# Strassen-type block products in a decoder layer: activation sums made in place and earlier, weight sums made by adding DMA transfers

## The chip, the cores and the metric

The kernel runs on one core of one Trainium2 chip. The metric is the device time of one execution in microseconds (us).

## The reference

One layer with two token mixers, in float32, for 1024 tokens and a model width of 1024:

```python
h = rmsnorm(x, ln_pre)
(c_val, c_glu, c_gate, q, k, v, a_gate, g_conv, g_attn) = split_columns(h @ w_in)
u = c_val * sigmoid(c_glu)
c = silu(layernorm(depthwise_causal_conv31(u) + b_dw))
ya = (c @ w_pw * silu(c_gate)) @ w_br_conv
yb = (sliding_window_sink_attention(q, k, v) * silu(a_gate)) @ w_br_attn
m = sigmoid(g_conv) * ya + sigmoid(g_attn) * yb
x = x + rmsnorm(m @ w_out, ln_post)
x = x + sigmoid(x @ w_ple_gate) * (p @ w_ple_proj)
```

The change lies around one of these products, `c @ w_pw`.

## The kernel before

**Products.** Activations lie transposed, with features on the partitions (8 blocks of 128) and the 1024 tokens along the row. Every float32 operand is split into two parts, `hi` (ScalarE copies it to fp32r) and `lo` (VectorE subtracts `hi` from the original), and TensorE makes three passes, hi·hi, lo·hi and hi·lo. A tile is 128 output features by 1024 tokens: 8 blocks of K, 3 passes, 2 halves, 48 matmuls of 128x512. Its weights (512 KB) are loaded by SyncE into `w_raw` with two slots, split into `w_hi` and `w_lo`, and its result goes to one of two slots of the PSUM tensor `psg`. Tiles are numbered: E0 = 58 to 65 is the product with `w_br_attn` (operand `o_hi`, `o_lo`), G0 = 66 to 73 that with `w_br_conv` (operand `y_hi`, `y_lo`), then `w_out` and `w_ple_gate`.

**The seven products.** Between tile 65 and tile 66 stands `c @ w_pw`. It is done by Strassen's scheme in Winograd's form: for each of four pairs of output tiles (`i` = 0 to 3) seven half-size products instead of eight, in the order P1, P2, P6, Q5, P7, Q3, P4, which are numbered b = 7i + n with n = 0 to 6 (`seventh`, L901 to L923). Each has 12 matmuls. P1, P2 and P4 use quarters of the activations (`c_hi`, `c_lo`), the four others sums of quarters (`s_hi`, `s_lo`). P1, P2 and Q3 use a block of the weights as loaded (`pair_raw`, 1 MB for each pair, SyncE, L497), the others sums of two to four blocks.

**Who makes what in this stage.**
- `row_sum` (VectorE, L1869 to L1881): four sums of quarters, 128x2048 each, from `conv` into `s_raw`. `s_raw` and the parts made from it lie where `o_hi` and `o_lo` lie, the operands of tile 65, so the sums wait until that tile has used them (`o_used`, `tile_done`). `sum_high` (ScalarE, L1259) and `row_low` (VectorE, L1883) split them.
- `pair_sum` (VectorE, L1838): four sums of weight blocks for each pair, 128x512 each.
- `block_high` (ScalarE, L1247) and `block_low` (VectorE, L1856): the two parts of each of the 28 weight operands, into `pair_w` with six slots. A slot is free when the product six before (three before in the last pair) is done.
- `keep` (ScalarE, L1264): copies a product out of PSUM where the next product in its bank adds to a copy. P6 waits for keep(P1), P7 for keep(P6), Q3 for keep(Q5) and P4 for keep(P7) (`kept_ready`, L917).
- `take` (VectorE, L1888): combines products, multiplies by the gate and writes `y_raw`. `y_high` and `y_low` split `y_raw` for tile 66.
- `merge_row` (VectorE, L1829): takes the result of a tile of the stage before out of PSUM.

**What sets the order.** It is written out by hand: a list of calls for ScalarE (L1284 to L1330) and one for VectorE (L1908 to L1974), each executed strictly in order, each instruction with its semaphore waits. A call that waits holds back all calls behind it on its engine. In the loop over b from 7 to 27, the `keep` calls of finished products (`made_since`) stand between the `block_high` calls. GpSimd has no work between 723 and 990 us of the span.

## Time and profile before

| | us |
|---|---|
| median of 3 runs | 1168.77 (1167.45 to 1169.88) |
| the profiled execution | 1169.1 |
| its span, first to last instruction | 1167.3 |
| TensorE busy in the span | 1152.7 (99%) |
| mean granted clock of TensorE | 0.995 of full speed |

The span stands for one execution; 1.8 us of that execution's time lie around it. Engines are PE (TensorE), PEld (its weight loads), DVE (VectorE), ACT (ScalarE), POOL (GpSimd) and SP (SyncE). "L919" is line 919 of the kernel. The number in brackets behind an instruction is the time its engine was idle before it, with what released it. "x2" means two instructions merged into one row, with the time from the start of the first to the end of the second.

### The profile page before, as it was taken

The page shows a single profiled execution, that of the slowest core. Times are in us where ns is not written, and L with a number is a line of the kernel's source. Part 1 is how long each engine was busy: PE and PEld are TensorE (multiplying, and loading weights), DVE is VectorE, ACT ScalarE, POOL GpSimd, SP SyncE. Part 2 cuts the span into 40 slices and gives each one's busy share as a digit, 9 for nine tenths or more (in the row PEclk, how much of TensorE's full clock was granted, in tenths as well). Part 3 has the DMA queues.
Part 4 walks back from the last instruction along what each step waited for, and adds up shares of the span by engine and source line. Part 5 has one row for each costly group of instructions (what it writes and reads, how often), then busy time and mean ns, then how long its engine had stood idle before and what let it go on. Part 6 is the DMA issues. An engine that isn't in the chain of part 4 may idle for free.

```text
span 1167.3 us, 16052 instructions
## 1 busy us (share of the span) xinstructions
PE 1152.7 (99%) x6256; PEld 938.7 (80%) x6256; DVE 900.1 (77%) x1025; ACT 398.8 (34%) x711; POOL 18.0 (2%) x16
## 2 busy tenths in 40 slices
PE   9999999999999999999999999999799999999998
PEld 7888888888888888877777888888687888888887
DVE  6999999999999984699886787867856444357776
ACT  6431221221221121366665433433334212344342
POOL 2020000000000000000000000000000000000000
PEclk9999999999999999999999999999899999999999
DMA  9622222222222323211212111453315432434565
GB/s 350 274 90 72 62 82 72 68 76 72 72 72 72 99 54 86 54 56 56 74 55 75 36 54 50 119 209 109 118 63 171 171 108 75 141 109 144 174 204 180
DMA packets 37408, 124.87 MB, mean 107 GB/s; under 512 B 4688, under 2 KB 5456, under 8 KB 36848
## 3 DMA queue, kind: packets, MB, share of 16 engines
q1 hardware_dynamic: 25840, 86.48, 23.0%
q10 hardware_dynamic: 11520, 37.75, 9.4%
q8 instruction: 30, 0.49, 0.2%
q14 instruction: 18, 0.15, 0.0%
HBM read 96.30 MB, written 25.17 MB: 104 GB/s over the span
## 4 chain that ended last, share of the span: by engine, by line
PE 93%; DVE 4%; ACT 2%; issue 1%; DMA 1%; ACTq 0%; SPq 0%; DVEq 0%
PE psg L555 72%; PE psg L847 6%; PE psb L919 5%; PE psg L579 2%; PE psb L761 1%; PE psg L818 1%; PE psg L662 1%; PE psg L608 1%; DVE s_raw L1881 1%; PE psg L779 1%; ACT probs L1134 1%; PE psg L813 1%; PE psb L662 1%; DMA p_raw<-pT 1%; PE psg L944 0%
## 5 line engine op out<-in xcount | busy, mean ns | idle before, releaser
L555 PE MATMUL psg<-h_hi,w_hi 128*128 128x512 f32 x768 | 236.9, 390 | 0.0
L555 PE MATMUL psg<-h_lo,w_hi 128*128 128x512 f32 x768 | 236.5, 389 | 0.0
L555 PE MATMUL psg<-h_hi,w_lo 128*128 128x512 f32 x768 | 236.4, 389 | 0.0
L1409 DVE TENSOR_TENSOR w_lo<-w_raw,w_hi 128x1024 fp32r<-128x1024 f32 x105 | 128.4, 1223 | 89.7 <-ACT w_hi L990 84.9
L555 PEld LDWEIGHTS psg<-h_hi,w_hi 128*128 128x128 f32 x768 | 143.9, 188 | 30.5 <-issue 0.8
L555 PEld LDWEIGHTS psg<-h_lo,w_hi 128*128 128x128 f32 x768 | 144.2, 188 | 29.9
L555 PEld LDWEIGHTS psg<-h_hi,w_lo 128*128 128x128 f32 x768 | 144.2, 188 | 29.9
L990 ACT ACTIVATE w_hi<-w_raw 128x1024 fp32r<-128x1024 f32 x104 | 110.0, 1058 | 165.0 <-PE psg L555 138.2
L1586 DVE SCALAR_TENSOR_TENSOR conv<-u,cols,conv 128x1024 f32<-128x1024 f32 x120 | 154.3, 1286 | 0.0
L1586 DVE SCALAR_TENSOR_TENSOR work<-u,cols,work 128x1024 f32<-128x1024 f32 x112 | 145.8, 1301 | 0.0
L847 PE MATMUL psg<-h_hi,w_hi 128*128 128x512 f32 x128 | 51.8, 405 | 0.0
L847 PE MATMUL psg<-h_hi,w_lo 128*128 128x512 f32 x128 | 49.9, 390 | 0.0
L847 PE MATMUL psg<-h_lo,w_hi 128*128 128x512 f32 x128 | 49.9, 390 | 0.0
L555 PE MATMUL psg<-x_hi,w_hi 128*128 128x512 f32 x120 | 46.7, 389 | 0.0
L555 PE MATMUL psg<-x_hi,w_lo 128*128 128x512 f32 x120 | 46.7, 389 | 0.0
L555 PE MATMUL psg<-x_lo,w_hi 128*128 128x512 f32 x120 | 46.7, 389 | 0.0
L555 PE MATMUL psg<-m_hi,w_hi 128*128 128x512 f32 x112 | 43.7, 390 | 0.0
L555 PE MATMUL psg<-m_lo,w_hi 128*128 128x512 f32 x112 | 43.6, 389 | 0.0
L555 PE MATMUL psg<-m_hi,w_lo 128*128 128x512 f32 x112 | 43.6, 389 | 0.0
L1980 DVE SCALAR_TENSOR_TENSOR work<-ring,psg 128x1024 f32<-128x1024 f32 x8 | 9.8, 1221 | 43.5 <-PE psg L555 38.8
L555 PE MATMUL psg<-y_hi,w_hi 128*128 128x512 f32 x128 | 40.0, 394 | 2.7 <-DVE w_lo L1409 2.7
L919 PE MATMUL psb<-s_hi,pair_w 128*128 128x512 f32 x128 | 39.7, 391 | 1.1 <-DVE pair_w L1864 1.1
(285 smaller groups left out, 1812.9 us busy)
## 6 DMA issues: line engine op xcount, KB each, us to landing
w_raw<-weights SPq DMA_DIRECT2D x106, 512.0 KB, 3.5
gates<-ring ACTq DMA_DIRECT2D x24, 512.0 KB, 2.7
ring<-gates ACTq DMA_DIRECT2D x24, 512.0 KB, 4.0
x_rows<-x_rows SPq DMA_DIRECT2D x8, 512.0 KB, 9.9
conv<-xT SPq DMA_DIRECT2D x8, 512.0 KB, 14.1
ple<-ple_out SPq DMA_DIRECT2D x8, 512.0 KB, 13.2
merged<-merged_out ACTq DMA_DIRECT2D x8, 512.0 KB, 5.3
pair_raw<-w_pairs SPq DMA_DIRECT2D x4, 1024.0 KB, 6.1
```

The lines of the kernel that those rows point to most:

```text
L555: mm = nc.tensor.matmul(psg[:, slot, h * HALF:(h + 1) * HALF], w[:, wslot, (wk + k) * P:(wk + k + 1) * P], r[:, k, h * HALF:(h + 1) * HALF ...
L579: mm = nc.tensor.matmul(psg[:, slot, h * HALF:(h + 1) * HALF], w[:, slot, k * P:(k + 1) * P], r[:, k, h * HALF:(h + 1) * HALF], start=(k = ...
L608: mm = nc.tensor.matmul(psg[:, slot, cols_h], w[:, slot, k * P:(k + 1) * P], r[:, k, cols_h], start=(k == 0 and n == 0), stop=(k == KT - 1 ...
L662: mm = nc.tensor.matmul(out, w[:, t // 4, cols_k], r[:, k, h * HALF:(h + 1) * HALF], start=(k == 0 and n == 0), stop=(k == PLE_KT - 1 and ...
L761: mm = nc.tensor.matmul(psb[out_rows, 2 * jp + par, j2 * 2 * P + first:j2 * 2 * P + first + width], qo[rows, 4 * g + 2 * jp + j2, queries] ...
L779: mm = nc.tensor.transpose(psg_banks[:, bank, first + h * HD:first + h * HD + HD], probs[g][queries, 4 * jp + h, :], ident[queries, queries])
L813: nc.tensor.matmul(out_of(p, side, par), vstep[rows, n - 1, gs], heads_of(pt_prev[rows], par), start=True, stop=False)
L847: mm = nc.tensor.matmul(gate_bank(p), w[:, t % 2, k * P:(k + 1) * P], r[:, k, half], start=(k == 0 and m == 0), stop=(k == KT - 1 and m == 2))
L919: mm = nc.tensor.matmul(psb[:, pair_bank(i, n), :], pair_w[:, at_w, w, k * P:(k + 1) * P], r[:, block_of, k, :], start=(not onto and k == ...
L990: nc.scalar.activation(w_hi[:, j % 2, :], w_raw[:, j % 2, :], ACT.Copy).then_inc(w_hi_ready, 1)
L1409: nc.vector.tensor_tensor(w_lo[:, slot, :], w_raw[:, slot, :], w_hi[:, slot, :].bitcast(F32), ALU.subtract).then_inc(w_lo_ready, 1)
L1586: own.step(stt(dst, src[:, j:j + S], tap(j), dst, ALU.mult, ALU.add))
```

## The change

1. **Activation sums in place.** `s_raw` is gone. The four `row_sum` calls write over the quarters of `conv` themselves, after the parts of `conv` have been made (`lo_ready` 3·KT), and so no longer wait for tile 65. They move ahead of tile 65, two before the `merge_row` of tile 63 and two before that of tile 64. Only the splits (`sum_high`) wait for tile 65's operands. The sums are used in the order P6, Q5, P7, Q3 as they are split. `c_high(7)` and `c_low(7)` move forward by one tile.
2. **Boundary steps reordered.** The lists of ScalarE and VectorE between tile 65 and b = 7 are written anew. The merge of tile 65 and the load of the second gate row now come before the splits of weights 4 to 6. At the end of the stage the split of tile 66's weights moves forward, to behind b = 24 (ScalarE) and b = 25 (VectorE), and the waits of `y_high` on products are one lower for two of four pairs.
3. **Weight sums by adding transfers.** `pair_sum` and its 16 instructions on VectorE are gone. GpSimd issues DMA transfers from the memory to four buffers of 128x512 (256 KB each): the first of a sum copies a block, each later one adds a block to what is there (`accum_op`). A pair needs 11 of them, 4 copies and 7 additions: P6 one copy and two additions, Q5 and P7 one and one, P4 one and three. Each addition waits for the transfer before it into the same buffer, each copy for the `block_low` that read the buffer for the pair before. All 44 transfers stand in one list on GpSimd's queue, the first behind `ln_scaled`.

```diff
-        s_raw = at("s_raw", [4, KP, HALF], F32, RD)
...
+        SUM_OF = {Q5: 0, P6: 1, P7: 2, P4: 3}
+        ADDENDS = ((0, 1), (0, 1, 3), (1, 3), (0, 1, 3, 2))
...
+        upper, lower = slice(0, HALF), slice(HALF, S)
+        def sum_of(n):
+            return conv[:, slice(KP, KT) if n in (1, 3) else slice(0, KP), upper if n in (0, 3) else lower]
...
+            def sum_step(i, n, step):
+                t = SUM_OF[n]
+                if step == 0 and i > 0:
+                    pool.wait_ge(pair_lo, 7 * (i - 1) + n + 1)
+                if step > 0:
+                    pool.wait_ge(sum_loaded[t], 16 * (len(ADDENDS[t]) * i + step))
+                op = ALU.bypass if step == 0 else ALU.add
+                pool.dma_start(pair_sums[t][:], WPW[:, i, ADDENDS[t][step], :], accum_op=op).then_inc(sum_loaded[t], 16)
+            pool.wait_ge(ln_scaled, KT)
+            for i in range(PAIRS):
+                sum_step(i, P6, 0)
+                sum_step(i, Q5, 0)
+                sum_step(i, P6, 1)
+                sum_step(i, Q5, 1)
+                sum_step(i, P6, 2)
+                sum_step(i, P7, 0)
+                sum_step(i, P4, 0)
+                sum_step(i, P7, 1)
+                sum_step(i, P4, 1)
+                sum_step(i, P4, 2)
+                sum_step(i, P4, 3)
             rsqrt(3, slice(0, NB // 2))
...
-                    act.wait_ge(pair_summed, 4 * i + {Q5: 1, P6: 2, P7: 3, P4: 4}[n])
-                    src = pair_sums[:, {Q5: 0, P6: 1}[n], :] if n in (Q5, P6) else pair_t[:, pair_slot(b), 1, :]
+                    t = SUM_OF[n]
+                    act.wait_ge(sum_loaded[t], 16 * len(ADDENDS[t]) * (i + 1))
+                    src = pair_sums[t][:]
...
-                act.wait_ge(s_made, n + 1)
-                nc.scalar.activation(s_hi[:, n], s_raw[:, n], ACT.Copy, scale=0.5).then_inc(s_hi_ready, 1)
+                act.wait_ge(s_made, 4)
+                if n < 3:
+                    act.wait_ge(o_used, n + 1)
+                else:
+                    act.wait_ge(tile_done, G0 + KT)
+                nc.scalar.activation(s_hi[:, n], sum_of(n), ACT.Copy, scale=0.5).then_inc(s_hi_ready, 1)
...
-                act.wait_ge(product_made, LAST_PAIR + (4, 4, 6, 6)[k // 2])
+                act.wait_ge(product_made, LAST_PAIR + (3, 4, 5, 6)[k // 2])
...
                 block_high(b)
+                if b == LAST_PAIR + Q5:
+                    high(G0 // 2 - 1, 2)
...
+                s2, s1, s3, s4 = (sum_of(j) for j in range(4))
+                a, b, op = {1: (s3, s1, ALU.subtract), 2: (s2, s3, ALU.subtract),
+                            0: (s1, s2, ALU.subtract), 3: (s4, s2, ALU.add)}[n]
+                dve.wait_ge(lo_ready, 3 * KT)
...
                 block_low(b)
+                if b == LAST_PAIR + P7:
+                    tile_low(G0)
             y_low(0)
             y_low(1)
+            take(PAIRS - 1, 1)
             y_low(2)
+            take(PAIRS - 1, 2)
             y_low(3)
-            take(PAIRS - 1, 1)
-            tile_low(G0)
-            take(PAIRS - 1, 2)
-            y_low(4)
-            y_low(5)
             take(PAIRS - 1, 3)
-            y_low(6)
-            y_low(7)
+            for k in range(KP, KT):
+                y_low(k)
...
-    nc = bacc.Bacc("TRN2", target_bir_lowering=False, num_devices=1, dynamic_dma_scratch_size=1024)
+    nc = bacc.Bacc("TRN2", target_bir_lowering=False, num_devices=1, dynamic_dma_scratch_size=2048)
```

VectorE from the merge of tile 63 on, before (`merged_out` is the merge of a tile, `s_raw` a row sum, `s_lo` its split, `pair_w` a block_low):

```order
L1836 SCALAR_TENSOR_TENSOR merged_out<-ring,psg 128x1024 [waits merged_spilled1,gate_loaded1,tile_done]
L1409 TENSOR_TENSOR w_lo<-w_raw,w_hi 128x1024 [waits w_hi_ready]
L1823 SCALAR_TENSOR_TENSOR c_lo<-conv,c_hi 128x2x512 [waits hi_ready]
L1853 TENSOR_TENSOR pair_sums<-pair_raw_83 128x512 [waits pair_loaded0]
L1853 TENSOR_TENSOR pair_sums<-pair_sums,pair_raw_83 128x512 [waits pair_summed,pair_loaded0]
L1836 SCALAR_TENSOR_TENSOR merged_out<-ring,psg 128x1024 [waits merged_spilled0,gate_loaded0,tile_done]
L1864 TENSOR_TENSOR pair_w<-pair_raw_83,pair_w 128x512 [waits pair_hi] x2
L1881 TENSOR_TENSOR s_raw<-conv 128x2048 [waits o_used]
L1881 TENSOR_TENSOR s_raw<-s_raw,conv 128x2048 [waits s_made,o_used]
L1886 SCALAR_TENSOR_TENSOR s_lo<-s_raw,s_hi 128x2048 [waits s_hi_ready]
L1881 TENSOR_TENSOR s_raw<-conv,s_raw 128x2048 [waits s_made,o_used]
L1886 SCALAR_TENSOR_TENSOR s_lo<-s_raw,s_hi 128x2048 [waits s_hi_ready]
```

The same place in the changed kernel (the in-place sums read `conv<-conv`, 128x4x512):

```order
L1860 SCALAR_TENSOR_TENSOR c_lo<-conv,c_hi 128x2x512 [waits hi_ready] x2
L1895 TENSOR_TENSOR conv<-conv 128x4x512 [waits lo_ready]
L1895 TENSOR_TENSOR conv<-conv 128x4x512 [waits s_made,lo_ready]
L1873 SCALAR_TENSOR_TENSOR merged_out<-ring,psg 128x1024 [waits merged_spilled1,gate_loaded1,tile_done]
L1446 TENSOR_TENSOR w_lo<-w_raw,w_hi 128x1024 [waits w_hi_ready]
L1895 TENSOR_TENSOR conv<-conv 128x4x512 [waits s_made,lo_ready] x2
L1873 SCALAR_TENSOR_TENSOR merged_out<-ring,psg 128x1024 [waits merged_spilled0,gate_loaded0,tile_done]
L1884 TENSOR_TENSOR pair_w<-pair_raw_83,pair_w 128x512 [waits pair_hi] x2
L1900 SCALAR_TENSOR_TENSOR s_lo<-conv,s_hi 128x2048 [waits s_hi_ready]
L1884 TENSOR_TENSOR pair_w<-pair_sums_115,pair_w 128x512 [waits pair_hi]
L1900 SCALAR_TENSOR_TENSOR s_lo<-conv,s_hi 128x2048 [waits s_hi_ready] x2
L1873 SCALAR_TENSOR_TENSOR merged_out<-ring,psg 128x1024 [waits merged_spilled1,gate_loaded1,tile_done]
```

All four row sums now stand ahead of the merge of tile 64, and no addition of weight blocks is left on VectorE.

ScalarE of the changed kernel from the split of weight 7 on (`pair_w` is a block_high, of b = 7 and 8, 9, 10, 11, 12, 13; `kept` are keep(P7 of pair 0) and keep(P1 of pair 1); `pair_sums_115` is the buffer of P6, 114 that of Q5, 116 that of P7, 117 that of P4):

```order
L1289 ACTIVATE pair_w<-pair_raw_84 128x512 [waits pair_loaded1,product_made] x2
L1289 ACTIVATE pair_w<-pair_sums_115 128x512 [waits sum_loaded1,product_made]
L1308 ACTIVATE kept<-psb 128x512 [waits quarter_read,product_made]
L1289 ACTIVATE pair_w<-pair_sums_114 128x512 [waits sum_loaded0,product_made]
L1289 ACTIVATE pair_w<-pair_sums_116 128x512 [waits sum_loaded2,product_made]
L1289 ACTIVATE pair_w<-pair_raw_84 128x512 [waits pair_loaded1,product_made]
L1308 ACTIVATE kept<-psb 128x512 [waits quarter_read,product_made]
L1358 DMA ring<-gates 128x1024 [waits y_made]
L1358 DMA ring<-gates 128x1024
L1289 ACTIVATE pair_w<-pair_sums_117 128x512 [waits sum_loaded3,product_made]
```

The sequence of calls is that of before, but four of them for each pair now wait for a DMA transfer (`sum_loaded`) where they waited for VectorE (`pair_summed`), and `kept` stands behind the one for P6.

GpSimd of the changed kernel, the 11 transfers of pair 1 (before, its queue is empty here):

```order
L993 DMA pair_sums_115<-w_pairs 128x512 [waits pair_lo]
L993 DMA pair_sums_114<-w_pairs 128x512 [waits pair_lo]
L993 DMA pair_sums_115<-w_pairs 128x512 [waits sum_loaded1]
L993 DMA pair_sums_114<-w_pairs 128x512 [waits sum_loaded0]
L993 DMA pair_sums_115<-w_pairs 128x512 [waits sum_loaded1]
L993 DMA pair_sums_116<-w_pairs 128x512 [waits pair_lo]
L993 DMA pair_sums_117<-w_pairs 128x512 [waits pair_lo]
L993 DMA pair_sums_116<-w_pairs 128x512 [waits sum_loaded2]
L993 DMA pair_sums_117<-w_pairs 128x512 [waits sum_loaded3] x3
```

The queue is served in this order, so an addition that waits for its forerunner holds back all the others.

## Rows read from the trace of the kernel before

**Rows 1.** The page: busy time by engine over the span.

```profile
PE 1152.7 (99%) x6256; PEld 938.7 (80%) x6256; DVE 900.1 (77%) x1025; ACT 398.8 (34%) x711; POOL 18.0 (2%) x16
```

**Rows 2.** Busy time by stretch: engines in order, granted clock, DMA share, GB/s.

```profile
core 0: us, PE busy (x) PEld busy (x) DVE busy (x) ACT busy (x) POOL busy (x), PEclk, DMA share, GB/s
...
810.30:829.50 19.20, 17.12 (x73) 13.09 (x71) 17.63 (x16) 8.15 (x11) 0.00 (x0) 1.00 0.05 12
829.50:838.70 9.20, 4.99 (x13) 3.97 (x14) 7.56 (x12) 2.84 (x6) 0.00 (x0) 0.63 0.59 204
838.70:893.00 54.30, 54.30 (x241) 44.95 (x240) 31.10 (x45) 20.07 (x33) 0.00 (x0) 1.00 0.26 89
...
895.80:904.50 8.70, 5.96 (x20) 4.69 (x20) 7.46 (x10) 2.40 (x3) 0.00 (x0) 0.80 0.86 275
```

**Rows 3.** TensorE in order of time: start, duration, instruction, idle before it.

```profile
810.33 0.62 PE L919 MATMUL psb<-c_hi,pair_w 128*128 128x512 f32 x2
...
822.72 0.73 PE L919 MATMUL psb<-s_hi,pair_w 128*128 128x512 f32 x2 [1.12 <-DVE pair_w L1864]
...
833.71 1.19 PE L919 MATMUL psb<-c_hi,pair_w 128*128 128x512 f32 x2 [5.18 <-ACT kept L1272]
...
838.61 0.63 PE L919 MATMUL psb<-c_hi,pair_w 128*128 128x512 f32 x2
...
893.04 0.62 PE L919 MATMUL psb<-c_hi,pair_w 128*128 128x512 f32 x2
...
898.67 0.70 PE L555 MATMUL psg<-y_hi,w_hi 128*128 128x512 f32 x2 [2.74 <-DVE w_lo L1409]
...
904.46 0.62 PE L555 MATMUL psg<-y_hi,w_hi 128*128 128x512 f32 x2
```

**Rows 4.** VectorE in order of time, 773 to 825 us.

```profile
773.56 1.22 DVE L1809 TENSOR_TENSOR conv<-conv,sums 128x1024 f32<-128x1024 f32 x1
...
788.77 1.22 DVE L1836 SCALAR_TENSOR_TENSOR merged_out<-ring,psg 128x1024 f32<-128x1024 f32 x1 [5.38 <-PE psg L555]
...
799.65 1.22 DVE L1836 SCALAR_TENSOR_TENSOR merged_out<-ring,psg 128x1024 f32<-128x1024 f32 x1 [5.97 <-PE psg L555]
...
803.70 2.28 DVE L1881 TENSOR_TENSOR s_raw<-conv 128x2048 f32<-128x2048 f32 x1
...
822.59 2.28 DVE L1886 SCALAR_TENSOR_TENSOR s_lo<-s_raw,s_hi 128x2048 fp32r<-128x2048 f32 x1
824.79 0.68 DVE L1864 TENSOR_TENSOR pair_w<-pair_raw,pair_w 128x512 fp32r<-128x512 f32 x1
```

**Rows 5.** ScalarE in order of time, 800 to 834 us.

```profile
806.02 1.92 ACT L1262 ACTIVATE s_hi<-s_raw 128x2048 fp32r<-128x2048 f32 x1 [3.04 <-DVE s_raw L1881]
...
829.61 1.15 ACT L1257 ACTIVATE pair_w<-pair_raw 128x512 fp32r<-128x512 f32 x2 [2.81 <-DVE merged_out L1836]
...
832.99 0.58 ACT L1272 ACTIVATE kept<-psb 128x512 f32<-128x512 f32 x1
```

**Rows 6.** VectorE in order of time, 890 to 900 us.

```profile
893.60 2.36 DVE L1418 SCALAR_TENSOR_TENSOR y_lo<-y_raw,y_hi 128x1024 fp32r<-128x1024 f32 x2 [0.97 <-ACT y_hi L1279]
...
897.20 1.22 DVE L1409 TENSOR_TENSOR w_lo<-w_raw,w_hi 128x1024 fp32r<-128x1024 f32 x1
```

**Rows 7.** DMA issues of the whole run: size, median us from issue to landing.

```profile
w_raw<-weights SPq DMA_DIRECT2D x106, 512.0 KB, 3.5
...
x_ring<-xT ACTq DMA_DIRECT2D x16, 256.0 KB, 3.4
...
pack<-qo SPq DMA_DIRECT2D x12, 64.0 KB, 2.3
```

**Rows 8.** DMA issues between 803 and 832 us, same columns.

```profile
merged<-merged_out ACTq DMA_DIRECT2D x1, 512.0 KB, 7.4
```

**Rows 9.** The DMA queue of SyncE, 803 to 832 us.

```profile
827.56 0.33 SPq L497 DMA_DIRECT2D pair_raw<-w_pairs  x1
```

**Rows 10.** GpSimd, groups by line: busy us, mean ns of one.

```profile
L962 POOL TENSOR_TENSOR rstd<-mean_sq,expo 128x4 f32<-128x4 f32 x3 | 3.1, 1020 | 405.7 <-DVE mean_sq L1423 387.5 <-DVE mean_sq L1453 18.2
```

More of the change, by code:

```diff
@@ L158, in build @@
         quarter = at("quarter", [HALF], F32, G + 14 * KB)
-        pair_sums = at("pair_sums", [2, HALF], F32, G + 16 * KB)
+        pair_sums = [at(f"pair_sums{t}", [HALF], F32, G + (16, 18, 32, 34)[t] * KB) for t in range(4)]
         sums = at("sums", [S], F32, G + 16 * KB)
@@ L180, in build @@
         v_last = cols[:, COL_TAPS:COL_TAPS + P]
-        assert small <= G + 24 * KB and G + 32 * KB <= nc.sbuf_usable_end
+        assert small <= G + 24 * KB and G + 36 * KB <= nc.sbuf_usable_end
         psg = ctx.enter_context(nc.psum_tensor("psg", [P, 2, S], F32))
@@ L269, in build @@
         pair_loaded = [sem("pair_loaded0"), sem("pair_loaded1")]
-        pair_summed = sem("pair_summed")
+        sum_loaded = [sem(f"sum_loaded{t}") for t in range(4)]
         pair_hi = sem("pair_hi")
@@ L907, in seventh @@
                     pe.wait_ge(lo_ready, 3 * KT)
[L908 to L909 removed]
+                if i == 0 and n in (P6, Q5, P7, Q3):
+                    pe.wait_ge(s_ready, {P6: 1, Q5: 2, P7: 3, Q3: 4}[n])
                 if i > 1 and n == P1:
@@ L1836, in merge_row @@
                 stt(merged_out[:, j, :], ring[:, j, :], 1.0, psg[:, j, :], ALU.add, ALU.mult).then_inc(ps_free[j], 1)
-            def pair_sum(i, n):
-                blocks = pair_raw[i % 2]
-                dve.wait_ge(pair_loaded[i % 2], 16 * (i // 2 + 1))
-                if n == Q5:
-                    out, a, b = pair_sums[:, 0, :], blocks[:, 0, :], blocks[:, 1, :]
-                elif n == P6:
-                    dve.wait_ge(pair_summed, 4 * i + 1)
-                    out, a, b = pair_sums[:, 1, :], pair_sums[:, 0, :], blocks[:, 3, :]
-                elif n == P4:
-                    from_slot(dve, 7 * i + n)
-                    out, a, b = pair_t[:, pair_slot(7 * i + n), 1, :], pair_sums[:, 1, :], blocks[:, 2, :]
-                else:
-                    from_slot(dve, 7 * i + n)
-                    out, a, b = pair_t[:, pair_slot(7 * i + n), 1, :], blocks[:, 1, :], blocks[:, 3, :]
-                nc.vector.tensor_tensor(out, a, b, ALU.add).then_inc(pair_summed, 1)
             def block_low(b):
@@ L1926, in _ @@
             block_low(1)
-            row_sum(0)
-            row_sum(1)
             row_low(0)
-            row_sum(2)
+            block_low(2)
             row_low(1)
-            block_low(2)
-            row_sum(3)
+            row_low(2)
+            merge_row(KT - 1)
             block_low(3)
-            pair_sum(0, P7)
             row_low(3)
+            take(0, 0)
             block_low(4)
-            row_low(2)
             block_low(5)
-            pair_sum(0, P4)
             block_low(6)
-            merge_row(KT - 1)
-            take(0, 0)
             for b in range(7, 7 * PAIRS):
```

55 lines of the change are left out of this document (19 added, 36 removed).

## The prediction

> **What bounds the kernel.** I read the busy shares first: TensorE is busy 99% of the span, 1152.7 of 1167.3 us [rows 1]. An edit off TensorE can therefore win only what TensorE loses in idle time, or at a lowered clock, and 14.6 us of idle time are all there is. The busy time by stretch shows where that lies near the change: TensorE idles 2.1 us between 810.3 and 829.5, 4.2 us up to 838.7 and 2.7 us between 895.8 and 904.5, while the 54.3 us between are full [rows 2]. The granted clock is 1.00 (the 2.4 GHz level) in the first and third stretch, and 0.63 and 0.80 in the other two, so part of the time there was at 1.2 GHz.
>
> TensorE's own rows give the sizes [rows 3]. In the full stretch 20 products take 893.04 − 838.61 = 54.43 us, 2.72 each. The first pair of tiles runs from 810.33 to 838.61, 28.28 us for seven products that need 7 × 2.72 = 19.04: 9.24 us lost. Of these, 1.12 are a wait for a weight split on VectorE and 5.18 a wait for `kept`; behind the latter the product at 833.71 takes 4.90 us instead of 2.72, because the clock had fallen after the idle time. The last product ends at 893.04 + 2.72 = 895.76, tile 66 starts at 898.67 after a wait for `w_lo`, and its fourth block of K, due 3 × 1.36 = 4.08 us after 895.76, comes at 904.46: 4.62 us lost. Together **13.9 us**.
>
> The causes are on the two engines with lists. VectorE does four row sums of 2.28 us after 803.7, and is still at the splits at 822.59 [rows 4]; it merges tile 65 only then, ScalarE waits for that merge until 829.61 with the later splits and the `kept` copy at 832.99 queued behind [rows 5], and that copy releases the product at 833.71. At the end `w_lo` stands behind four `y_lo` splits and ends at 898.4 [rows 6].
>
> **Part 1, sums in place and sooner.** Two row sums and one `c_lo` (2 × 2.28 by the row of a sum, 1.22 for the split, together 5.8 us) go ahead of the merge at 788.77, which had 5.38 us of idle time before it; two sums (4.5) go ahead of the merge at 799.65, which had 5.97 and loses two weight sums besides [rows 4]. The first merge may come 0.3 us late; TensorE needs its slot only one tile later, so I charge nothing. If that cover were gone, the price would be what exceeds the 10.9 us of a tile (4 × 2.72).
>
> After tile 65 I walk through the new lists. Behind the merge that starts at 799.65 and two DMA issues, ScalarE splits three weight blocks in some 0.55 each (two took 1.15) from 801.8, and row sums in 1.92 each from 803.4 [rows 5]. VectorE splits of 2.2 (822.59 to 824.79) then end at 807.5, 810.3, 812.5 and, behind the merge of tile 65 and block_low(3) (done at 814.3), at 816.5 [rows 4]. The products that use them are due at 815.8, 818.5, 821.2 and 823.9. block_low(4) ends at 818.4 against 821.2. The tightest spare is 2.8 us. So all 9.24 us go, if the weight sums arrive.
>
> **Part 2, the end of the stage.** `w_hi` and `w_lo` of tile 66 are now made behind splits 24 and 25, several microseconds ahead of 895.76, and `y_lo` of block k is needed only at 895.76 + 1.36 k, where VectorE needs 1.2 us each. All 4.62 us go.
>
> **Part 3, adding transfers.** VectorE loses 16 sums of 0.69 us; it has idle time there, so nothing on the path. What is added is a chain on GpSimd's queue, and no row shows one: GpSimd issued no transfer before, and no transfer added.
>
> Prices. *Issue*: SyncE's takes 0.33 us [rows 9], GpSimd's smallest two-operand instruction 1.02 [rows 10]; I take 1.0, since the same engine has to prepare 128 rows. *Copy* of 256 KB, issue to landing: 2.3 us for 64 KB and 7.4 for a transfer in a crowded stretch are the ends [rows 7, 8]; I take 3.4, the row of the same size. *Addition*: the same ends; I take the copy plus the time for reading a second 256 KB, by (3.5 − 2.3) / 448 KB × 256 KB = 0.7, so 4.1 us.
>
> The Trainium skill (Collectives: The Full Stack, the section on the bandwidth ceiling) says that a reducing transfer is slowed by reading two sources and not by the addition. No run here shows it yet; a doubling of the data part alone is what my 0.7 supposes.
>
> The queue is served in order, so one pair takes: P6 copy 3.4, first P6 addition 4.1, issue 1.0, P7 copy 3.4, issue 1.0, P4 additions 4.1 and 4.1, issue 1.0. That is **22.1 us for each pair, against 19.04 that TensorE takes**. The chain thus falls behind by 3.1 us a pair, from a lead it has at the start.
> - Pair 0: issued from the last `ln_scaled` at 774.8 [rows 4] on, landed by some 801, needed from 802 on, the last after 819. No wait.
> - Pair 1: the second transfer, a copy for Q5, waits for block_low(3) at 814.3 and holds back the rest. P6 is summed at 814.4 + 1.0 + 4.1 + 4.1 = 823.6. ScalarE then splits it (0.5) and copies P7 (0.5): `kept` stands ready at 824.7, P4 is due at 810.33 + 6 × 2.72 = 826.65. No wait. The turn ends at 834.1.
> - Pair 2: P6 summed at 834.1 + 3.4 + 8.2 = 845.7, `kept` at 846.8, P4 of pair 1 due at 845.7: **1.1 us**. P4's sum lands at 859.3, and keep(P6) behind it at 860.9 against 860.4: **0.5 us**.
> - Pair 3: turn from 856.2, P6 summed at 867.8, `kept` at 868.9, P4 of pair 2 due at 866.3: **2.5 us**, and behind a wait of that size the clock falls: 4.90 − 2.72 = 2.2 and 4.62 − 2.91 = 1.7 were lost at the lower level [rows 3], so **2.0**. P4's sum lands at 881.4, due at about 892.
>
> **The sum**: 1169.1 (the profiled execution: span 1167.3 and 1.8 around it; 0.3 above the median of 1168.77) − 13.9 + 1.1 + 0.5 + 2.5 + 2.0 = 1161.3. Against the median 1161.0.
>
> **Rivals.**
> - *The chain keeps up.* With a turn under 20 us no product waits. A copy of 2.8 (between the rows of 64 and 512 KB) and an addition of 3.5 give 5.6 + 10.5 + 3.0 = 19.1. Then 1169.1 − 13.9 = 1155.2. For it: the DMA engines are busy only 26% between 838.7 and 893 [rows 2]. Against it: 33 transfers of 262 kB add 8.7 MB to the 4.8 MB of these 54 us, and the additions read their target too. The Trainium skill (DMA: Bandwidth & Descriptors, the section on the anatomy of one DMA from gpsimd) gives 2.0 us plus bytes over 436 GB/s, an estimate of 2.6 us for a copy here; by that the sum would be this rival's. No run here shows it yet.
> - *Slower: keep(P7) behind the weight split.* ScalarE cannot copy P7 out of its bank before it has split the next pair's P6 sum, and TensorE's P4 waits for that copy. With additions of 6.1 us (a little above half way from 4.1 to the crowded 7.4) P6 of pair 1 is summed at 827.6, P4 of pair 0 waits 2.0 us, and a turn takes 28.1: by the same walk four more waits of 2.5 us follow, each behind the same kind of wait, and all five drop the clock. 12 + 5 × 2.0 = 22 us, against 13.9 saved: 1177.2. It decides from additions of about 5.3 us on (turn 25.7). For it: transfers compete with 1 MB of `pair_raw` and 1 MB of gates in each pair, and a transfer in such company took 7.4 [rows 8]. Against it: that one wrote to memory, and twice the data. With 7.4 for an addition the same walk gives 1189.
> - *The change doesn't do all it says.* If sums in place held a merge up by a tile or the boundary kept a wait, some microseconds of 9.24 would stay. The walk shows 2.8 us spare; small.
>
> **Chances.** The chain a little late, as in my sum: 0.35. It keeps up: 0.27. Additions near 5.3 us, both effects cancelling: 0.11. Slower through late sums: 0.24. A boundary wait that stays: 0.03. A change of 0.2%, 2.3 us, is about what a measurement can tell from none. Faster 0.64, same 0.12, slower 0.24. The likeliest case alone spans 1156 to 1166. The range goes from 1154.5, the rival without any wait less a little, to 1178, the slower rival; additions beyond some 6.1 us are left out, with a chance of about 0.13.
>
> **What would show it.** In the changed kernel's profile the waits at P7 of pair 0 (1.12), P4 of pair 0 (5.18) and tile 66 (2.74) should be gone, and four row sums should stand before 800 us. GpSimd's transfers of `pair_sums` should land 3.4 to 4.1 us after issue and repeat every 22 us; waits on `kept` should be seen at P4 of pairs 1 and 2, with ScalarE's `pair_w` of P6 released by a DMA. No such waits at all would mean the first rival, a wait already at P4 of pair 0 the second. I would be wrong altogether if TensorE waited for `s_lo` or if the merge of tile 63 moved by more than a microsecond.

## The result and the profile after

The changed kernel takes **1184.47 us** (median of 4 executions, 1183.57 to 1186.32) against 1169.09 for the kernel before in the same series: a ratio of 1.0135, 95% interval 1.0118 to 1.0153. It is slower by 15.4 us, and 1161.0 with a range up to 1178 had been forecast. The profiled execution took 1186.32 us with a span of 1184.5, 17.2 above the span of before.

The page of the changed kernel, the lines that answer to [rows 1] and [rows 7], and TensorE's waits in the stage:

```profile
PE 1159.9 (98%) x6256; PEld 942.9 (80%) x6256; DVE 889.6 (75%) x1009; ACT 398.4 (34%) x711; POOL 52.3 (4%) x60
...
L926 PE MATMUL psb<-s_hi,pair_w 128*128 128x512 f32 x128 | 42.5, 415 | 6.5 <-ACT kept L1308 6.5
L926 PE MATMUL psb<-c_hi,pair_w 128*128 128x512 f32 x96 | 34.6, 446 | 13.0 <-ACT kept L1308 13.0
...
pair_sums<-w_pairs POOLq DMA_DIRECT2D x44, 256.0 KB, 5.3
```

The same matrix work is now busy for 7.2 us longer (1159.9 against 1152.7), which is lowered clock, and 19.5 us of idle time stand before the products, all of it behind `kept`. The 44 transfers land a median 5.3 us after issue.

The stage by stretch, with the columns of [rows 2], two of six stretches and the sum of all:

```profile
810.30:829.40 19.10, 16.58 (x74) 13.39 (x72) 10.82 (x12) 7.35 (x11) 4.37 (x6) 1.00 0.81 215
...
860.00:880.00 20.00, 16.74 (x60) 13.30 (x60) 5.77 (x9) 3.92 (x7) 4.68 (x6) 0.83 0.65 163
...
sum 107.20, PE 87.70 PEld 69.88 DVE 43.70 ACT 31.65 POOL 25.00; mean PE 14.62 PEld 11.65 DVE 7.28 ACT 5.28 POOL 4.17
```

TensorE in order of time, answering to [rows 3]: the first product, the fifth and the seventh (P7 and P4 of pair 0), P4 of pair 3, and tile 66.

```profile
810.40 0.62 PE L926 MATMUL psb<-c_hi,pair_w 128*128 128x512 f32 x2
...
821.28 0.62 PE L926 MATMUL psb<-s_hi,pair_w 128*128 128x512 f32 x2
...
830.25 0.70 PE L926 MATMUL psb<-c_hi,pair_w 128*128 128x512 f32 x2 [3.37 <-ACT kept L1308]
...
913.18 1.17 PE L926 MATMUL psb<-c_hi,pair_w 128*128 128x512 f32 x2 [3.17 <-ACT kept L1308]
...
917.59 0.62 PE L562 MATMUL psg<-y_hi,w_hi 128*128 128x512 f32 x2
```

From 810.40 to 917.59 the 28 products take 107.2 us where 28 × 2.72 = 76.2 are needed: **31.0 us are lost**, against 13.9 before. The difference of 17.1 is the whole difference of the spans (17.2), so nothing of the loss lies elsewhere. TensorE is busy 87.7 of the 107.2 us: 19.5 us are idle (six waits, of 3.37, 4.62, 4.46, 1.87, 2.02 and 3.17 us) and 11.5 are work at a lowered clock (0.83 to 0.91 in the mean of each stretch from 829.4 us on, where the steady part of before has 1.00).

Parts 1 and 2 did what they should. The fifth product comes in step (810.40 + 4 × 2.72 = 821.28), where the first pair of before had its first wait; tile 66 starts without one. What is left is part 3. ScalarE in order of time shows the wait that releases P4 of pair 0:

```profile
829.00 0.63 ACT L1289 ACTIVATE pair_w<-pair_sums 128x512 fp32r<-128x512 f32 x1 [5.88 <-DMA pair_sums<-w_pairs]
829.53 0.58 ACT L1308 ACTIVATE kept<-psb 128x512 f32<-128x512 f32 x1
...
837.62 0.82 ACTq L1358 DMA_DIRECT2D ring<-gates  x2
```

The split of pair 1's P6 sum waits 5.88 us for its DMA, and the copy of P7, done by TensorE at 824.0, stands behind it until 829.53. The other waits are of two kinds. Those at P4 of pairs 1 and 2 are like this one. Those at P7 of pairs 1 and 2 and at P4 of pair 3 stand behind the split of a P4 sum: in pair 1 it waits 10.37 us for its DMA (848.57), with keep(P6) behind it at 849.63. And GpSimd's queue in order of time shows why the sums are late (each row is one to three issues; in brackets the landing that let them go):

```profile
808.09 1.45 POOL L993 DMA_DIRECT2D pair_sums<-w_pairs  x2 [4.62 <-DMA pair_sums<-w_pairs]
814.74 1.50 POOL L993 DMA_DIRECT2D pair_sums<-w_pairs  x2 [5.21 <-DVE pair_w L1884]
...
837.96 0.86 POOL L993 DMA_DIRECT2D pair_sums<-w_pairs  x1 [6.22 <-DMA pair_sums<-w_pairs]
844.32 2.00 POOL L993 DMA_DIRECT2D pair_sums<-w_pairs  x3 [5.50 <-DMA pair_sums<-w_pairs]
850.23 1.81 POOL L993 DMA_DIRECT2D pair_sums<-w_pairs  x2 [3.90 <-DMA pair_sums<-w_pairs]
857.14 2.00 POOL L993 DMA_DIRECT2D pair_sums<-w_pairs  x3 [5.11 <-DMA pair_sums<-w_pairs]
863.46 1.82 POOL L993 DMA_DIRECT2D pair_sums<-w_pairs  x2 [4.31 <-DMA pair_sums<-w_pairs]
870.35 0.86 POOL L993 DMA_DIRECT2D pair_sums<-w_pairs  x1 [5.06 <-DMA pair_sums<-w_pairs]
874.92 1.99 POOL L993 DMA_DIRECT2D pair_sums<-w_pairs  x3 [3.71 <-DMA pair_sums<-w_pairs]
880.52 1.85 POOL L993 DMA_DIRECT2D pair_sums<-w_pairs  x2 [3.62 <-DMA pair_sums<-w_pairs]
885.01 2.00 POOL L993 DMA_DIRECT2D pair_sums<-w_pairs  x3 [2.63 <-DMA pair_sums<-w_pairs]
891.74 1.82 POOL L993 DMA_DIRECT2D pair_sums<-w_pairs  x2 [4.73 <-DMA pair_sums<-w_pairs]
900.19 0.86 POOL L993 DMA_DIRECT2D pair_sums<-w_pairs  x1 [6.63 <-DMA pair_sums<-w_pairs]
904.65 0.88 POOL L993 DMA_DIRECT2D pair_sums<-w_pairs  x1 [3.60 <-DMA pair_sums<-w_pairs]
```

A turn of the chain, from the last addition of one pair's P4 to that of the next, takes 36.2 us at first (with 5.21 of waiting for the `block_low` that frees Q5's buffer), then **30.6** (844.32 to 874.92) and 29.7 (874.92 to 904.65), against 19.04 for TensorE's seven products. It consists of five hops, each from one release to the next. Beside the prediction's terms for the same hops, the differences of neighbouring rows are:

| hop | of the same list in flight beside it | forecast | second turn | third turn |
|---|---|---|---|---|
| copy for P6 | P4's last addition, the copy for Q5 | 4.4 | 5.91 | 5.60 |
| first addition for P6 | the addition for Q5 | 4.1 | 6.91 | 4.49 |
| copy for P7 | P6's second addition, the copy for P4 | 4.4 | 6.32 | 6.73 |
| first addition for P4 | the addition for P7 | 5.1 | 6.89 | 8.45 |
| second addition for P4 | none | 4.1 | 4.57 | 4.46 |
| turn | | 22.1 | 30.6 | 29.7 |

In these two turns every row is let go by a landing, none by a `block_low`, so the buffers hold nothing up. The one addition with nothing of the list beside it is 0.4 us dearer than forecast; of the eight hops in company, seven are 1.2 to 3.4 us dearer. Other loads may weigh on it too: in the first turn the last hop took 844.32 − 837.96 = 6.36 us, where ScalarE had just issued 1 MB of gates (837.62); no run changes these loads alone.

Set against the chain, the loss reads as follows. P4 of pair 0 was due at 810.40 + 6 × 2.72 = 826.72, 18.6 us behind the issue of its last addition (808.09); P4 of pair 3 starts 8.5 us behind its own (913.18, 904.65). So 10.1 us of lead are used up. The three turns take 96.6 us where TensorE needs 57.1, 39.4 more. 39.4 − 10.1 = 29.3, and the last product takes 4.41 us instead of 2.72 at the lowered clock: 31.0. This balance must close whatever the cause, since it only splits the time between two products.

So it is a reading, not yet a proof: an addition may be dear for itself, and the order of the lists or the buffers may hold the chain. The experiments take it apart.

### The profile page after: what moved, and what is told of

Read it like the earlier page. It is cut to its first block, busy times and chain, and to the rows that moved or that the text cites. A ratio compares the mean times of both kernels' runs of the same rounds, so it can differ in the third digit from the quotient of the medians.

```text
span 1184.5 us, 16074 instructions
## 1 busy us (share of the span) xinstructions
PE 1159.9 (98%) x6256; PEld 942.9 (80%) x6256; DVE 889.6 (75%) x1009; ACT 398.4 (34%) x711; POOL 52.3 (4%) x60
## 4 chain that ended last, share of the span: by engine, by line
PE 88%; DMA 7%; DVE 2%; ACT 1%; issue 1%; POOL 0%; ACTq 0%; SPq 0%; DVEq 0%; POOLq 0%
PE psg L562 71%; PE psg L854 6%; DMA pair_sums<-w_pairs 6%; PE psb L926 2%; PE psg L586 2%; PE psb L768 1%; PE psg L825 1%; DMA conv<-xT 1%; PE psg L615 1%; PE psg L786 1%; ACT probs L1165 1%; PE psg L820 1%; DVE s_lo L1900 1%; PE psg L951 0%; PE psg L669 0%
## 5 line engine op out<-in xcount | busy, mean ns | idle before, releaser
L1884 DVE TENSOR_TENSOR pair_w<-pair_sums,pair_w 128x512 fp32r<-128x512 f32 x16 | 11.0, 689 | 58.4 <-ACT pair_w L1289 58.4
L926 PE MATMUL psb<-s_hi,pair_w 128*128 128x512 f32 x128 | 42.5, 415 | 6.5 <-ACT kept L1308 6.5
L926 PE MATMUL psb<-c_hi,pair_w 128*128 128x512 f32 x96 | 34.6, 446 | 13.0 <-ACT kept L1308 13.0
L993 POOL DMA_DIRECT2D pair_sums<-w_pairs x44 | 34.3, 923 | 222.4 <-DVE conv L1846 126.3
```

Source lines behind the costliest of these rows:

```text
L926: mm = nc.tensor.matmul(psb[:, pair_bank(i, n), :], pair_w[:, at_w, w, k * P:(k + 1) * P], r[:, block_of, k, :], start=(not onto and k == ...
L993: pool.dma_start(pair_sums[t][:], WPW[:, i, ADDENDS[t][step], :], accum_op=op).then_inc(sum_loaded[t], 16)
```

## The experiments

All were run beside the kernel before. Theory A: parts 1 and 2 give back the 13.9 us, and the chain of transfers is the bound and costs 31. The rivals: the moved steps cost something that the chain hides; adding transfers disturb other engines or loads by themselves; the chain is late through its order, through buffers, or through the order on ScalarE.

### Weight sums on VectorE again, parts 1 and 2 kept

The 44 transfers are gone; VectorE forms the four sums of a pair in one go, those of pair 0 ahead of the merge of tile 64, the later ones behind the last `block_low` of the pair before.

```diff
...
+            def pair_sums_of(i):
+                blocks = pair_raw[i % 2]
+                dve.wait_ge(pair_loaded[i % 2], 16 * (i // 2 + 1))
+                if i > 0:
+                    dve.wait_ge(pair_lo, 7 * i)
+                for n, a, b in ((Q5, blocks[:, 0, :], blocks[:, 1, :]), (P6, pair_sums[0][:], blocks[:, 3, :]),
+                                (P7, blocks[:, 1, :], blocks[:, 3, :]), (P4, pair_sums[1][:], blocks[:, 2, :])):
...
                 block_low(b)
+                if b % 7 == P4 and b < LAST_PAIR:
+                    pair_sums_of(b // 7 + 1)
```

> The changed kernel with part 3 undone: the weight sums are made by VectorE again, the four of a pair together behind the split of P4 of the pair before, into the changed kernel's four buffers. Parts 1 and 2 stay. Theory A (the chain of landings on GpSimd's queue is the whole loss): all waits of the stage go, 13.9 us less than before, about 1155 us, ratio 0.988. Rival B (parts 1 and 2 do not save what the walk says, for instance because VectorE is late again with four more sums before tile 64's merge): a wait of some microseconds stays at P7 or P4 of the first pair, 1158 to 1164.

Measured: 1155.42 us (1154.78 to 1155.75), ratio 0.9885 (0.9868 to 0.9901), span 1153.0. The first stretch of its stage:

```profile
810.30:829.40 19.10, 19.10 (x86) 15.81 (x85) 17.48 (x23) 9.28 (x15) 0.00 (x0) 1.00 0.35 111
```

TensorE is busy every microsecond, at a clock of 1.00. The span is 14.3 us under that of before, and the median 13.4 us under that of its own series (1168.81), around the 13.9 that parts 1 and 2 were to win. Part 3, put on top of them, costs 1184.47 − 1155.42 = 29 us by the medians, 31.5 between the two profiled spans. This version beats both kernels.

### The old boundary lists, and the old end of the stage

Two kernels made from the one above, each with one piece of the reordering undone. In the first, the lists of ScalarE and VectorE between tile 65 and b = 7 stand in the order of before the change, without the row sums and weight sums that stood there (the cut shows VectorE's):

```diff
             row_low(0)
-            block_low(2)
             row_low(1)
-            row_low(2)
-            merge_row(KT - 1)
+            block_low(2)
             block_low(3)
-            row_low(3)
-            take(0, 0)
+            row_low(2)
             block_low(4)
+            row_low(3)
             block_low(5)
             block_low(6)
+            merge_row(KT - 1)
+            take(0, 0)
...
```

> e1 with the order of the boundary lists of before (second gate row and merge of tile 65 behind the splits of weights 4 to 6), but the activation sums still in place and early. Tells part 1 from the reordered boundary steps. Theory A, by a walk through the lists: with the sums away, block_low(6) ends about 821 and the merge of tile 65 behind it, keep(P7) is 1.4 us late, too short for the clock to fall: 1156.5 to 1157.5, so that nearly all of the 9.2 us belong to the early sums. Rival E (the order of the lists is what counts): 1160 or more.

Measured: 1157.20 us (1157.09 to 1157.75), 0.9902 (0.9885 to 0.9918). One wait comes back, at P4 of pair 0:

```profile
828.45 0.70 PE L927 MATMUL psb<-c_hi,pair_w 128*128 128x512 f32 x2 [1.58 <-ACT kept L1286]
```

So the new lists are worth 1.8 us. By difference the other 7.4 of the first pair's 9.24 come from what has left these lists: above all the four row sums of 2.28 us, now ahead of tile 65, but in this kernel also the two weight sums of 0.69 us. No run puts the row sums back alone. In the second, the end of the stage is the old one:

```diff
...
-                if b == LAST_PAIR + P7:
-                    tile_low(G0)
             y_low(0)
             y_low(1)
-            take(PAIRS - 1, 1)
             y_low(2)
-            take(PAIRS - 1, 2)
             y_low(3)
+            take(PAIRS - 1, 1)
+            tile_low(G0)
...
```

> e1 with the end of the stage as before: the split of tile 66's weights behind four y splits again. Theory A: the wait of 2.7 us at tile 66 and the slow matmuls behind it come back, 4.6 us, 1160.0. Rival D (with VectorE's lists changed the split is no longer late): 1155 to 1157.

Measured: 1157.95 us (1157.53 to 1160.13), 0.9912 (0.9896 to 0.9929). Tile 66 waits again, for nearly the same time as before (2.74 in [rows 3]), and its fourth block follows at the full rate:

```profile
888.98 0.70 PE L563 MATMUL psg<-y_hi,w_hi 128*128 128x512 f32 x2 [2.37 <-DVE w_lo L1423]
...
893.16 0.62 PE L563 MATMUL psg<-y_hi,w_hi 128*128 128x512 f32 x2
```

893.16 − 888.98 = 4.18 us for three blocks, where [rows 3] have 5.79. So the wait returned without the 1.7 us of lowered clock behind it, and the piece is worth 1157.95 − 1155.42 = 2.5 us in this surrounding, not 4.6. In the kernel before, the clock was back at 1.00 for 54 us ahead of that wait too [rows 2]; why it fell there and not here, these runs don't show.

### The same 44 transfers, all as copies

The chain, its waits and its bytes read stay; the additions become plain copies. The weight sums are thereby left out of the computation.

```diff
-                op = ALU.bypass if step == 0 else ALU.add
+                op = ALU.bypass
```

> The changed kernel with every adding transfer turned into a plain copy of the same block, so that the sums of weights are left out; number, size, order and waits of the transfers stay. Theory A1 (an addition costs much more than a copy because it reads its target too): landings fall from a median of 5.3 to about 4 us, a turn from 30 to about 23 us, the time to about 1163. Rival A2 (transfers from this queue are slow as such, by preparation and crowding): landings stay above 5 us, the time above 1178.

Measured: 1163.53 us (1162.26 to 1164.51), 0.9953 (0.9937 to 0.9968); transfers land after 2.9/3.7/7.6 us (least, median, most). Its waits, and one stretch:

```profile
PE psb L926 <- ACT kept L1308: 6.6, 4, 2.7
```

```profile
860.00:880.00 20.00, 18.50 (x81) 14.68 (x81) 7.25 (x11) 4.36 (x8) 5.52 (x11) 1.00 0.61 216
```

GpSimd's queue, the last addition's place of pairs 1, 2 and 3 (a plain copy here):

```profile
835.78 0.54 POOL L993 DMA_DIRECT2D pair_sums<-w_pairs  x1 [2.65 <-DMA pair_sums<-w_pairs]
...
859.66 1.59 POOL L993 DMA_DIRECT2D pair_sums<-w_pairs  x3 [2.70 <-DMA pair_sums<-w_pairs]
...
881.45 0.54 POOL L993 DMA_DIRECT2D pair_sums<-w_pairs  x1 [3.57 <-DMA pair_sums<-w_pairs]
```

A chain with the same list and only copies still makes TensorE wait 6.6 us and costs 1163.53 − 1155.42 = 8.1 us; adding costs 1184.47 − 1163.53 = 20.9 us more. So of the 29 us of part 3 the larger share is the price of adding, at the same number of transfers and the same bytes read from the memory. The turns are 23.9 us (835.78 to 859.66) and 21.8 (859.66 to 881.45), where the changed kernel has 30.6 and 29.7. In the stretch shown the DMA engines move 216 GB/s at a busy share of 0.61; the changed kernel moves 163 at 0.65.

The clock behind these waits went both ways: behind the longest, 2.69 us at P4 of pair 0, it fell (0.65 in the mean from 829.1 to 834.0), behind 2.37 us at P4 of pair 1 it stayed at 1.00. In the changed kernel it fell behind 1.87 us (0.67 from 881.3 to 886.5) and stayed at 1.00 behind 2.02 us (from 890.6 to 895.0). The length of the wait alone does not decide it.

### Transfers timed by themselves

The first kernel of this section again, with trial transfers between 88 and 195 us, where GpSimd has no other work: five single copies and five single additions of 256 KB, four and four of 64 KB, four times two copies at once into two buffers, four times two additions.

```diff
...
+            def one(t, op, width=HALF, wait=True):
+                if wait:
+                    pool.wait_ge(trial[t], 16 * done[t])
+                pool.dma_start(pair_sums[2 + t][:, 0:width], WPW[:, 0, t, 0:width], accum_op=op).then_inc(trial[t], 16)
+                done[t] += 1
...
```

> e1 with transfers that serve no purpose between 90 and 400 us, when only the weight loads run: on GpSimd's queue, each waiting for the one before, 5 copies and 5 additions of 256 KB, 4 copies and 4 additions of 64 KB, then 4 pairs of copies and 4 pairs of additions of 256 KB, two at once. Gives the quiet prices. Theory A1: copy 3 to 3.5 us, addition 4 to 5, two at once little more. Rival A2: copy and addition both at 4 us or above, two at once clearly more (6). The time of the kernel should be that of e1.

GpSimd in order of time; a trial lasts from its row to the next: single copies from 98.90, single additions from 110.01, two copies at once from 156.56, two additions at once from 171.13.

```profile
98.90 0.54 POOL L991 DMA_DIRECT2D pair_sums<-w_pairs  x1 [2.73 <-DMA pair_sums<-w_pairs]
102.12 0.54 POOL L991 DMA_DIRECT2D pair_sums<-w_pairs  x1 [2.68 <-DMA pair_sums<-w_pairs]
...
110.01 0.88 POOL L991 DMA_DIRECT2D pair_sums<-w_pairs  x1 [3.62 <-DMA pair_sums<-w_pairs]
114.44 0.86 POOL L991 DMA_DIRECT2D pair_sums<-w_pairs  x1 [3.55 <-DMA pair_sums<-w_pairs]
...
156.56 1.06 POOL L991 DMA_DIRECT2D pair_sums<-w_pairs  x2 [4.13 <-DMA pair_sums<-w_pairs]
160.90 1.06 POOL L991 DMA_DIRECT2D pair_sums<-w_pairs  x2 [3.28 <-DMA pair_sums<-w_pairs]
...
171.13 1.80 POOL L991 DMA_DIRECT2D pair_sums<-w_pairs  x2 [3.73 <-DMA pair_sums<-w_pairs]
177.92 1.77 POOL L991 DMA_DIRECT2D pair_sums<-w_pairs  x2 [4.99 <-DMA pair_sums<-w_pairs]
184.80 1.81 POOL L991 DMA_DIRECT2D pair_sums<-w_pairs  x2 [5.11 <-DMA pair_sums<-w_pairs]
192.92 1.77 POOL L991 DMA_DIRECT2D pair_sums<-w_pairs  x2 [6.31 <-DMA pair_sums<-w_pairs]
```

Issue to next issue, so with the issue in it: a copy of 256 KB 3.2 to 3.6 us (98.90 to 102.12: 3.22; one of five took 4.1), an addition **4.4 to 4.7** (110.01 to 114.44: 4.43); of 64 KB 2.4 to 3.1 and 2.9 to 3.6. Two copies at once 4.3 to 5.4 (156.56 to 160.90: 4.34), two additions at once **6.8, 6.9 and 8.1**. GpSimd needs 0.54 us to issue a copy and 0.87 for an addition. The time was 1154.95 us (one execution), so the trials cost nothing there. Single issues of additions in the stage of the changed kernel take the same 0.86 to 0.91 us, so what is dearer in company is the way from issue to landing.

A single addition is thus 1.1 us dearer than a copy, 0.33 of it in the issue. The second of two concurrent additions adds 2.4 us or more, the second of two concurrent copies 1 to 2. On the reason, the Trainium skill (Collectives: The Full Stack, the section on the bandwidth ceiling) says of ReduceScatter that it is slowed by the second source read and not by the addition. That an addition is dearer here agrees in direction, but no run splits the two. The Trainium skill's fit (DMA: Bandwidth & Descriptors, the anatomy of one DMA from gpsimd) gives an estimate of 2.6 us for a copy of 256 KB; measured are 3.2 to 3.6, so the measurement decides. The rival in which the chain keeps up took 2.8 for a copy and 3.5 for an addition, too little by 0.4 to 0.8 and 0.9 to 1.2 us.

### Two of the four sums by transfers

Q5 and P7, one copy and one addition each, stay with GpSimd; the longer sums of P6 and P4 go to VectorE.

```diff
+            for i in range(PAIRS):
+                sum_step(i, Q5, 0)
+                sum_step(i, P7, 0)
+                sum_step(i, Q5, 1)
+                sum_step(i, P7, 1)
```

> Half of part 3: the sums of Q5 and P7 (one copy and one addition each) stay with GpSimd's transfers, two copies together, then two additions; P6 and P4 are summed by VectorE. Theory A (what decides is a turn of the chain against TensorE's 19.04 us a pair): two landings with two transfers in flight, by the trials 5 us for copies and 7 for additions, some 12 to 13 us a turn, so no wait and the time of e1, 1155 to 1156. Rival C (adding transfers hurt by themselves, by delaying the other transfers or the engines, about 0.7 us for each of 28 additions by the 29 us between the changed kernel and e1): 16 transfers less crowded, still 4 to 8 us above e1.

Measured: 1155.06 us (1154.94 to 1155.36), 0.9883 (0.9866 to 0.9899); landings 2.8/5.0/8.9 us. No product waits:

```profile
840.00:860.00 20.00, 20.00 (x90) 16.58 (x89) 11.26 (x17) 7.33 (x13) 2.90 (x4) 1.00 0.51 134
```

Landings are as slow as in the changed kernel, and cost nothing: two landings a pair fit into 19 us, five of them don't. Eight adding transfers beside full TensorE work do no harm by themselves; what does harm is a chain of dependent hops. (The expectation spreads the 29 us wrongly: they are 0.7 us for each of 44 transfers, or 1.0 for each of 28 additions, so rival C asked for up to 8 us more here. The measured time, 0.4 us under that of the first kernel of this section, excludes it either way.) It gains nothing over VectorE's sums either, which were off the path.

### Fewer landings in a turn

The list of a pair is written so that four buffers move together: four copies, four first additions, two second, one third. That makes four dependent landings instead of five.

```diff
+                for n, step in ((P6, 0), (P4, 0), (Q5, 0), (P7, 0), (P6, 1), (P4, 1), (Q5, 1), (P7, 1), (P6, 2), (P4, 2), (P4, 3)):
+                    sum_step(i, n, step)
```

> The changed kernel with the 11 transfers of a pair in another order: the four copies together, then the four first additions, then the second ones of P6 and P4, then the third of P4: four landings behind one another in a turn instead of five. If a landing took the same 5.5 to 6 us with four in flight, a turn would fall from 30 to about 24 us and the time to about 1170. If the landings grow with the number in flight (the queue or the engines are shared), a turn stays near 30 and the time near 1184 or above, since P6's sum would come later in its turn.

Measured: 1183.00 us (1182.22 to 1183.78), 1.0120 (1.0100 to 1.0140): a miss, as good as no gain. GpSimd in order of time, one turn:

```profile
820.96 2.54 POOL L993 DMA_DIRECT2D pair_sums<-w_pairs  x4 [11.74 <-DVE pair_w L1875]
...
848.79 2.54 POOL L993 DMA_DIRECT2D pair_sums<-w_pairs  x4 [9.38 <-DVE pair_w L1875]
```

The turn is still 848.79 − 820.96 = 27.8 us. The transfers need some 18 of it; but the copy for P4, now second, must wait until the `block_low` of the P4 before has read the buffer (9.38 us idle), and that `block_low` stands behind steps of ScalarE that wait for the late TensorE (4.60 and 2.39 us idle from 838.6 to 846.2). P6's sum also comes later in its turn, so that TensorE's wait at P4 of pair 0 grows to 10.75 us. The chain's length was traded for a ring through the buffers.

### Copies from another queue

SyncE issues the 16 copies as early as the buffers allow, GpSimd only the 28 additions.

```diff
...
+            def start_sums(i):
+                for n in (P6, Q5, P7, P4):
+                    t = SUM_OF[n]
+                    if i > 0:
+                        sp.wait_ge(pair_lo, 7 * (i - 1) + n + 1)
+                    sp.dma_start(pair_sums[t][:], WPW[:, i, ADDENDS[t][0], :]).then_inc(sum_started[t], 16)
...
```

> The changed kernel with the first step of each sum, a plain copy, issued by SyncE, and only the 28 additions by GpSimd. The copies are then prefetched off the chain, and GpSimd's turn holds three landings instead of five. With 5.5 to 6 us each and three issues of 0.9 a turn takes 19 to 21 us, close to TensorE's 19.04: Theory A expects no wait at the first pair and 0 to 3 us later, 1156 to 1163. Rival F (the engines' crowding sets the pace and not the number of landings in a row; the bytes are the same): a turn of 27 us or more, above 1175.

Measured: 1166.76 us (1164.73 to 1169.62, 10 executions), 0.9983 (0.9973 to 0.9993): 18 us better than the changed kernel, 2 us below the time of before, and above what was expected. GpSimd's queue, and one row of SyncE's, in order of time:

```profile
810.92 0.88 POOL L1006 DMA_DIRECT2D pair_sums<-w_pairs  x1 [6.57 <-DMA pair_sums<-w_pairs]
821.21 3.55 POOL L1006 DMA_DIRECT2D pair_sums<-w_pairs  x4 [9.40 <-DMA pair_sums<-w_pairs]
...
837.60 2.65 POOL L1006 DMA_DIRECT2D pair_sums<-w_pairs  x3 [4.31 <-DMA pair_sums<-w_pairs]
...
861.03 2.67 POOL L1006 DMA_DIRECT2D pair_sums<-w_pairs  x3 [4.42 <-DMA pair_sums<-w_pairs]
```

```profile
814.10 0.33 SPq L522 DMA_DIRECT2D pair_sums<-w_pairs  x1
```

With the landings of the copies out of the chain a turn takes 861.03 − 837.60 = 23.4 us, 7 less. The first sum of pair 1 is late all the same. Its first addition goes at 810.92, but Q5's addition stands behind it in GpSimd's queue, and Q5's copy was only issued at 814.10, when its buffer came free, and landed 7.1 us later, beside 1 MB of gates and merged result. P6's second addition had to wait behind that. TensorE waits 4.5, 1.7 and 1.6 us. An order of additions without this hold was not tried.

### The copy of P7 ahead of the split

In the changed kernel the copy of P7 waits behind the split of the next pair's P6 sum. Here it stands ahead of it for pairs 0 to 2.

```diff
...
+                if b % 7 == P6 and b < LAST_PAIR:
+                    keep(b // 7 - 1, P7)
+                    kept_early.append((b // 7 - 1, P7))
                 block_high(b)
```

> The changed kernel with one call of ScalarE moved: for pairs 0 to 2 the copy of P7 out of its bank (kept) stands ahead of the split of the next pair's P6 sum instead of behind it. All 44 transfers stay. Theory A (the chain of transfers is the bound; the copy behind the split only decides which product feels it first): the wait at P4 of pair 0 (3.4 us at 830.25) goes, but the chain's turns stay at 30 us from the block_low that it waits for at 814.7 on, so its last addition lands within 2 us of where it did and the time is 1183 to 1186 us, at most 3 us better. Theory B (the order on ScalarE is the cause, transfers are late only because TensorE is): each of the waits on kept of some 4 us goes with its drop of the clock, some 3 x 5 us, and the time is 1165 to 1172.

Measured: 1186.45 us (1185.41 to 1186.78), 1.0146 (1.0129 to 1.0163). TensorE's waits, and further down the last addition of the chain on GpSimd:

```profile
PE psb L926 <- ACT kept L1308: 22.7, 6, 7.1
```

```profile
905.42 0.88 POOL L993 DMA_DIRECT2D pair_sums<-w_pairs  x1 [3.68 <-DMA pair_sums<-w_pairs]
```

The wait at P4 of pair 0 is gone; the first is now at P6 of pair 1 and the largest at P7 of pair 1, 7.1 us. The last addition is issued at 905.42 against 904.65, and the time is that of the changed kernel within 2 us. The order on ScalarE only says which product feels the chain.

## Why the prediction was wrong

**What bounds the kernel, and parts 1 and 2: right.** 13.9 us were to come back, and the kernel with these parts alone is 13.4 us shorter by its medians and 14.3 by the spans. The walk through the lists held: VectorE's rows show two row sums ahead of the merge of tile 63 (the other two follow at 791.65), that merge 0.6 us late (0.3 forecast), and block_low(4) in its place.

```profile
784.78 4.69 DVE L1895 TENSOR_TENSOR conv<-conv 128x2048 f32<-128x2048 f32 x2
789.39 1.21 DVE L1873 SCALAR_TENSOR_TENSOR merged_out<-ring,psg 128x1024 f32<-128x1024 f32 x1
```

block_low(4) was due at 818.4 by the walk and ended at 818.6. Only the clock's share at tile 66, 1.7 of the 4.6 us, did not show when that wait was put back.

**Part 3, the frame: right.** The queue served in order, five dependent landings a turn, a turn against 19.04 us of TensorE, and `kept` behind the split of a P6 or P4 sum as the place where it is felt: all of it is in the rows. With copies alone, where the turn is 21.8 to 23.9 us, the loss is 8.1 us; the walk gave 6.1 for 22.1. Of the six waits measured it had three, P4 of pair 1, P7 and P4 of pair 2.

**The step that failed** is the price of a transfer in that chain: a copy at 3.4 us and an addition at 4.1, for a turn of 22.1. The copy was a median over the whole run, the addition that copy plus 0.7 worked out from two such medians. Measured with nothing but the weight loads beside them they are nearly right (3.2 to 3.6, and 4.4 to 4.7, both with the issue). But the list sends two or three at a time: in four of five hops something of the list is under way beside the one waited for, and in two of them that is a second addition, where two additions at once take 6.8 to 8.1 us. The turn is 30.6 and 29.7 and not 22.1 us, the lag for each pair 11.6 and 10.7 and not 3.1.

The kernel with copies alone splits the miss. By the prediction's terms a turn of copies is 5 × 3.4 + 3 × 1.0 = 20.0 us; measured are 22.84 in the mean of two. Adding was to cost 3 × 0.7 = 2.1 us a turn; measured are 30.16 − 22.84 = 7.3 (30.16 is the mean of the changed kernel's second and third turn). So of the 8.1 us missing in a turn 2.8 belong to copies in company and 5.2 to adding. Two hops with two additions at once explain some 2 × 2.3 of the 7.3, and the single one 1.1 (an estimate from the trials: 7.3 against 5.0 us in the mean for two at once); the rest are copies beside additions, which no trial times. Why the second addition is so dear stays open.

The one row that showed a transfer in company, 7.4 us [rows 8], was taken as the far end, because it was twice the size and wrote to memory; it was the nearest row in what mattered, the company. A smaller point is the clock: the prediction took it that a wait of 2.5 us makes it fall. It fell behind five of the six waits, but not behind that of 2.02 us.

**The rivals.** The slower one was the right one in kind: its first wait was to be at P4 of pair 0 (2.0 us; 3.4 measured), behind the same copy, with a wait and a drop of the clock in every pair. It was too small, since it made only the additions dear (6.1) and left the copies at 3.4: 28.1 against 30.6 a turn, 22 us lost against 31. That is also why its limit was misplaced. It was to decide from additions of 5.3 us on; the median landing was 5.3, and the kernel was 15 us slower, because the hops of copies, too, took 5.6 to 6.7. With the measured loss in its place the sum is 1169.1 − 13.9 + 31.0 = 1186.2, the profiled execution's 1186.3; that only says that the loss lies in this stage. The rival without any wait was out of reach: even with copies alone TensorE waited 6.6 us.

**The range** ended at the slower rival's own time, with a chance of 0.13 beyond it. With prices for company of 7.4 us at hand, the 1189 of that end belonged inside.
